# Moving five adaLN steps from the change of layers behind blocks of the second layer's input projection

## What is computed

```python
mod = silu(cond) @ w_ada[l] + b_ada[l]              # 6 vectors of 1024: sh1, sc1, g1, sh2, sc2, g2
hn = rmsnorm(x, norm_mix[l]) * (1 + sc1) + sh1
proj = hn @ w_in[l]                                  # 1024 x 3840
mix = concat(diff_attention, retention, hgrn2)(proj) # three groups of heads
x = x + g1 * (mix @ w_out[l])
hn = rmsnorm(x, norm_ffn[l]) * (1 + sc2) + sh2
x = x + g2 * moe(hn)                                 # 16 experts, top 2 inside the best group of 4
```

## Time and profile before

| | before |
|---|---|
| median of 3 runs | 951.84 us (951.6 to 954.29) |
| span of the profiled execution | 949.4 us |
| PE busy | 917.2 us, 97% of the span |
| PE's share of the chain that ended last | 82% |
| DVE busy | 431.7 us, 45% |
| ACT busy | 158.6 us, 17% |
| loads of SP's queue | 291.52 MB |
| mean granted clock of TensorE | 0.994 |

### The profile page before, as it was taken

How to read it: one execution, slowest core, us unless ns; L and a number is a source line. 1 busy time by engine, 2 the same in 40 slices (tenths; PEclk the granted TensorE clock), 3 DMA queues, 4 the chain that set the end, 5 groups by cost and what they waited for, 6 DMA issues and landing times.

```text
span 949.4 us, 13394 instructions
## 1 busy us (share of the span) xinstructions
PE 917.2 (97%) x5191; PEld 498.8 (53%) x5197; DVE 431.7 (45%) x780; ACT 158.6 (17%) x408; POOL 63.6 (7%) x96
## 2 busy tenths in 40 slices
PE   5999999999899999999998999999999999999997
PEld 1655575678544444444437556657864444443442
DVE  1486887643423212222235999876252321222223
ACT  2211033321210010001111211533021001000100
POOL 1113130020000000000010224000000000000001
PEclk9999999999999999999999999999999999999999
DMA  9996574595999999999997432601099999999993
GB/s 365 412 401 255 216 268 191 231 327 202 420 421 421 421 422 420 421 421 422 419 419 300 157 109 91 246 21 46 28 376 421 421 420 422 420 421 421 420 421 135
DMA packets 48430, 303.63 MB, mean 320 GB/s; under 512 B 7680, under 2 KB 7696, under 8 KB 14960
## 3 DMA queue, kind: packets, MB, share of 16 engines
q1 hardware_dynamic: 42368, 291.52, 75.4%
q0 software_dynamic: 2960, 8.63, 2.5%
q10 hardware_dynamic: 3040, 2.62, 0.8%
HBM read 300.10 MB, written 2.65 MB: 319 GB/s over the span
## 4 chain that ended last, share of the span: by engine, by line
PE 82%; DVE 9%; DMA 4%; ACT 2%; issue 1%; SPq 1%; DVEq 0%; ACTq 0%
PE ps L428 80%; DMA wT<-in_w_in 4%; PE ps L462 2%; ACT eP L1583 1%; DVE fa L1264 1%; DVE stat L1058 1%; DVE rt L1058 1%; DVE eP L1362 1%; DVE xy L1258 1%; DVE eP L1360 1%; SPq L369 1%; DVE sq L1215 0%; DVE proj L1291 0%; DVE proj L1225 0%; DVE t L1281 0%
## 5 line engine op out<-in xcount | busy, mean ns | idle before, releaser
L428 PE MATMUL ps<-ring,proj 128*64 128x512 f32 x1024 | 226.3, 595 | 1.0 <-ACT proj L1830 1.0
L428 PE MATMUL ps<-ring,hnT 128*128 128x512 f32 (+1 forms) x576 | 202.1, 503 | 1.4 <-DVE hnT L1438 0.9
L428 PEld LDWEIGHTS ps<-ring,hnT 128*128 128x128 f32 x576 | 106.4, 190 | 74.3 <-issue 66.0
L428 PEld LDWEIGHTS ps<-ring,proj 128*64 128x64 f32 x1024 | 72.6, 137 | 132.8 <-issue 131.1
L428 PEld LDWEIGHTS ps<-proj,xs 128*128 128x128 f32 x512 | 58.4, 192 | 12.5 <-issue 11.4
L428 PE MATMUL ps<-proj 128*128 128x512 f32 x128 | 61.7, 607 | 0.0
L428 PE MATMUL ps<-proj,xs 128*128 128x128 f32 x512 | 61.4, 278 | 0.1
L1554 DVE COPY proj<-ps 128x512 f32<-128x512 f32 x16 | 11.1, 691 | 107.9 <-PE ps L428 107.9
L428 PE MATMUL ps<-fa,proj 128*64 128x512 f32 x128 | 57.5, 592 | 0.0
L428 PE MATMUL ps<-eP,proj 128*64 128x512 f32 x128 | 57.5, 592 | 0.0
L428 PE MATMUL ps<-wT,proj 128*64 128x512 f32 x128 | 57.5, 592 | 0.0
(11 more groups left out here) (235 smaller groups left out, 979.8 us busy)
## 6 DMA issues: line engine op xcount, KB each, us to landing
ring<-in_w_gate SPq DMA_DIRECT2D x64, 1024.0 KB, 15.2
ring<-in_w_down SPq DMA_DIRECT2D x64, 1024.0 KB, 17.5
ring<-in_w_ada SPq DMA_DIRECT2D x48, 1024.0 KB, 9.0
ring<-in_w_in SPq DMA_DIRECT2D x24, 1024.0 KB, 8.2
eP<-in_w_up SPq DMA_DIRECT2D x16, 1024.0 KB, 16.5
wT<-in_w_up SPq DMA_DIRECT2D x16, 1024.0 KB, 18.6
fa<-in_w_up SPq DMA_DIRECT2D x16, 1024.0 KB, 18.2
xy<-in_w_up SPq DMA_DIRECT2D x16, 1024.0 KB, 19.9
```

The source lines that it names most:

```text
L428: ins = nc.tensor.matmul(*a, **k)
```

## The change

The five steps leave the change of layers: their loads no longer stand ahead of block "f" in SP's order, and PE streams 18 matmuls of zeros in their place. All eight steps of pair "y" now stand behind blocks of the second layer's input projection: two behind "a", one behind "b", one behind "i" and four, instead of three, behind "r". The number of loads and steps stays the same; the ring slots that each load takes shift, as they are taken in turn.

```diff
-ADA_BEHIND = ((2, 3, 3, 3, 3, 2, 3, 2), (0, 0, 0, 0, 0, 3, 0, 0))
-AT_CHANGE = 5
+ADA_BEHIND = ((2, 3, 3, 3, 3, 2, 3, 2), (0, 0, 2, 1, 1, 4, 0, 0))
...
-                 [(1, "y", k) for k in range(AT_CHANGE, KC)]]
+                 [(1, "y", k) for k in range(KC)]]
         IN_ROUTER = [(1, "g", k) for k in range(KC)]
-        IN_CHANGE = [(1, "y", k) for k in range(AT_CHANGE)]
...
                 if l == 0:
                     for step in EARLY:
-                        load_ada(*step)
-                else:
-                    for step in IN_CHANGE:
                         load_ada(*step)
...
-                def at_change(b):
-                    for step in IN_CHANGE:
-                        ada_step(*step)
-
...
-                    normalized_group("hn1", "xn1", 0, at_change)
+                    normalized_group("hn1", "xn1", 0, lambda b: stream_zeros(b, 18))
```

## The result

The changed kernel takes 955.57 us (median; 954.10 to 958.66) against 952.50 us for the kernel before, measured again with it (950.74 to 955.21): a ratio of 1.0029 (95% interval 1.0020 to 1.0038). It is slower by 2.8 us. The forecast was +0.5 us, and the time lies above the range. 0.66 us of the distance to the forecast is the base: 951.84 was the median of three executions, 952.50 is that of twenty. The rest, +2.8 where +0.5 was forecast, is the change's.

A forecast was written before the change was run, and what follows sets the result against it. PE, busy 97% of the span, was taken as the bound. Terms -2.8 (change of layers), +4.5 (steps), -0.8 (stop at 552.7), -0.4 (slack at 613) gave +0.5 us: 952.3 us median, range 949.5 to 954.8.

The forecast's parts named there:

- The loads: Moved adaLN loads cost nothing; block f's load, issued ahead of them, lands at 487.8, 11 us before PE can use it.
- The change of layers, -2.8: Block f's first group ends at 503.0 instead of 505.82: 1.7 us of clock and 1.1 of earlier start.
- the 1.7 us of clock: First group of block f, 5.31 us against 3.59 for the second; this loss to the low clock was to be won back.
- the wait for wT: PE's 2.04 us stop ahead of block f until its load lands; hnT was to come last instead.
- The five steps, +4.5: Moved steps behind blocks of the second layer cost PE 0.90 us each, within 4.5 to 5.4 in all.
- Rival (5): A single step behind a block costs 1.07 us instead of 0.90: +0.9 more, 953.2; within the forecast's chance of 0.57.
- The stop at 552.7, -0.8: In the levels, PE's wait for a PSUM bank disappears because DVE frees the bank earlier, at 549.8.
- The slack at 613, -0.4: At the reduction over latent-token scores, products ready 0.4 us early absorb part of PE's delay; DVE ends at +0.5.
- Rivals (1): In block f the clock falls all the same, once, as long as now: price 1.7 us, 954.0; chance 0.14.
- Rival (2): Clock stays low longer, over the norm and second group too: +3.9 us, 955.7, slower; chance 0.08.
- rival (4): Block f is still late behind some other load, so the change of layers gives nothing: +3.3, 955.1; chance 0.03.
- The +2.2: Sum instead of +0.5 if, by the skill's rule on brief frequent idling, the clock gain at block f stays lost.

The follow-up runs named there:

- e3: Changed kernel without the matmuls of the five moved steps, their loads kept; 951.36 us, ratio to before 0.9984.
- e4: Kernel before with four steps at the change of layers, the fifth moved behind block r, no zeros; 951.92 us, ratio 0.9992.
- e10: Kernel before, unchanged, run again for a further trace; 951.63 us.
- e8: Kernel before with four steps at the change of layers, the fifth moved behind block a; 952.23 us, ratio 0.9991.
- e12: Kernel before with four steps at the change of layers and the fifth behind block a, measured once more; 951.91 us, ratio 0.9992.
- e1: Kernel before, unchanged, run again for a second trace; 953.52 us, ratio to itself 1.0005.
- e9: Kernel before, unchanged, run again for a further trace; 955.10 us.
- e11: Kernel before, unchanged, run again for a further trace; 952.64 us.
- e5: Kernel before with five zero matmuls streamed in the stop ahead of block f of the second layer; 952.19 us, ratio 0.9999.
- e7: Changed kernel with all eight steps of pair y behind block r; 964.32 us, ratio to before 1.0115.
- e6: Changed kernel without the 18 zero matmuls at the change of layers; 955.95 us, ratio to before 1.0034.

## Why the prediction was wrong, point by point

**The loads: right in what they cost.** "f" was issued before any adaLN load and PE waited for no load between 500 and 640. e3 shows that the moved loads cost nothing. The reading that "f" came late because SP issued it late doesn't hold: e4 and e10 show that the bytes ahead of wT set its landing, which is also how the prediction worked out the time.

**The change of layers, -2.8: the step that failed.** The runs show about -1.0 in its place. Against the trace from which it was worked out the sum came true: the stage shrank from 16.55 to 13.60 us, 2.95 instead of 2.8. But it was worked out from one execution, and that one isn't typical. In four further traces of before the stage takes 14.03 to 14.24. Against 13.61, the change wins 0.4 to 0.6 us in those, and 1.0 against the mean of all five (14.59). The times say the same: e3 is 1.5 us below before, and e4, e8 and e12 are 0.8 below it although their moved step costs 0.3 to 0.5, so 1.1 to 1.3, though each of these ratios is good to some 1.2 us to either side.

Two terms were priced as if every execution had them: the 1.7 us of clock, which no other trace of before shows, and the wait for wT, which is the difference of two arrivals. wT landed at 500.28 in the first trace and at 502.03 in e1; DVE began the diagonal at 495.80 and 498.19. In each of the six traces of this order of loads SP issues wT 6.2 us before the change of layers starts, and what differs is how long the load then takes: 14.50 us in the first trace, 13.85 in e1, 12.6 in e9. In e11, e10 and e9 it lands 7.5, 7.0 and 6.4 us behind the start. A likely reason is that every fall in the first layer puts PE back, while the stream of loads, limited by its bytes (421 GB/s), goes on. What speaks for it: the two traces without a fall between 251 and 260, the first and e5, are those with the latest wT, 8.3 and 9.2 us behind the start, and in the four with it the load lands 6.4 to 7.7 behind. No run tests it, and the order of the starts alone doesn't give it (e5 starts at 493.99, between the others). The load of wT in the chain of e1:

```profile
488.18 13.85 DMA wT<-in_w_in
```

I had seen that the DMA engines were saturated and that the clock fell at other places, and did not ask what either means for the next execution.

**The five steps, +4.5: right in kind, too small.** In the first trace of before the levels start at

```profile
545.43 2.00 PE L428 MATMUL ps<-xy 64*128 64x64 f32 x32
```

From the rows of after against this and the earlier trace rows, counted from the second group of "f": two steps behind a cost 2.06 us (the levels start 38.95 behind it instead of 36.89), the one behind b 1.00 (from one pair of levels to the next 6.56 instead of 5.56), the one behind i 1.09 (4.63 from the start of the block's last matmuls to the transposes instead of 3.54), the additional one in a row behind r 0.86. That is 5.0, inside the 4.5 to 5.4 that the prediction gave. Rival (5), the 1.07 of a single step, was nearer than the 0.90 of steps in a row, which I took as the value. Steps in a row do cost 0.88 (e7).

**The stop at 552.7, -0.8: right.** It is gone: from the pair of levels with the stop to the next, 5.56 us instead of 6.39.

**The slack at 613, -0.4: right.** PE is 4.15 us later there, counted from the second group of "f" (107.16 against 103.01), the reduction 3.81 (108.60 against 104.79), and it waits for PE 1.18 us. The forecast had 3.7 and 3.3 (from -2.8 to +0.9 and to +0.5). All of the 3.8 stays to the output projection (153.69 against 149.87 without a fall).

**The clock: falls come and go, and the rivals named the wrong place.** Rivals (1) and (2) looked for falls in "f" of the changed kernel; it had none there. (The prediction counts three short stops in place of a long one; that ahead of the second group, 0.67, stands in both kernels, so there are two.) It had one at 646 to 648 in both traces, where PE does 16 small products of modX and then stops for 0.61 us, and e7 has one at the same work (656); before has the same products, with stops of 0.3 to 0.6 us behind them, and no fall there in five traces. It has one at 630 to 632 in three of five, behind the stop of 1.2 us ahead of the attention's values, which stands in the other two as well. The price is the same 1.45 us. Why the place differs, and whether the changed kernel has its fall more often, two traces don't settle.

**The sum again**: -1.0 at the change (the mean of five traces), +5.0 for the steps, -0.8, -0.4: +2.8. With the 0.5 of the four like traces it is +3.3. Measured were 2.8 and 3.1 (1.0029 and 1.0032 of 952.5 and 952.9). Of the 2.3 us by which the forecast was too low, 1.8 are the change of layers and 0.5 the steps. How often executions like the first trace occur is open, and so is whether the fall at 648, in both traces of after, adds to the difference: before has its own in three of five.

Of the chances: rival (4), in which the change of layers gives nothing, came nearest in its difference, +3.3, though not for its reason. (Rival (2) has the nearest time, 955.7, because its difference of +3.9 was added to the lower base.) "f" was no longer late; it just is, in most executions, less late before than in the one that was read. The +2.2 that the prediction gives for the case that the 1.7 us of clock stay lost is close to what came, by luck: in the changed kernel PE ran at full clock from 500 to 510.

## What to carry to other kernels

The length of a wait is the difference of two arrivals. Where one comes from a stream of loads that is limited by its bytes and the other from an engine whose clock falls at varying places, take several traces before the wait is priced, or price it by its range; a clock fall behind it even more so. And where an engine is busy for 97%, work that sits beside a wait is hidden, while the same work elsewhere costs its full time: here 5.0 us put in, 3.8 paid. And what makes a load land late is the bytes ahead of it, where the DMA engines are saturated, more than the time of its issue: one load fewer ahead of wT brought it forward by its 2.5 us (e4), and four steps at the change did for "f" nearly what none did.

## What the runs showed of the hardware

The fall of the clock is no fixed event. At the change of layers, it followed on a stop of 2.04 us (first trace) and came within one of 4.13 us (e6), and not on 1.84 (e5), 1.39 (e1) and 1.25 (e11). Behind the stop of 1.2 us at 628 it fell in three traces of before and not in the other two. The Trainium skill (TensorE: Matmul & The Clock Gate, "HAM oscillation — how this bites in real kernels") has the clock go down on long waits between groups of matmuls, of 3 to 5 us in its example; the traces here have it down after shorter ones too, and differently from one execution to the next of the same program. The price of a fall can be less than PE's own loss: the one in e1, about 3.4 us at the lower level (5 us from 630 on at 0.66), costs 1.45 us, where half of 3.4 is 1.7. That DVE and ACT, which hold part of the chain there, take up the rest is argued, not measured.

Four f32 matmuls on 32 columns each, side by side, take 0.88 us per step in a row (e7). A step that stands alone between matmuls of the full width adds 1.0 to 1.2 us (behind b 1.00 and behind i 1.09 in the first trace of after, behind a 1.20 in e12).
